# A two-block transformer kernel: in the bidirectional scan, the carried part of the output is scaled on ScalarE and the order of VectorE's work in a scan step is rearranged

## The reference, cut to what matters

```
cb     = einsum("bclgn,bcsgn->bcgls", cm, bm)
y_diag = einsum("bcgls,bcgels,bcsgep->bclgep", cb, exp(segsum(a)), xs)
y_off  = einsum("bclgn,bcgepn,bcgel->bclgep", cm, prev_states, exp(a_cs))
y      = y_diag + y_off
```

## Time and profile before

| | |
|---|---|
| median of three runs | 3659.97 us |
| the profiled execution: its time | 3656.11 us |
| its span, first to last instruction | 3654.3 us |
| TensorE busy | 3439.4 us (94%) |
| VectorE busy | 2409.4 us (66%) |
| ScalarE busy | 1713.0 us (47%) |
| GpSimd busy | 492.3 us (13%) |
| the eight full steps of the scan | about 1984 to 2195 us |

### The profile page before, as it was taken

The page is one execution under the profiler, slowest core; times in us unless marked ns, Lnnn a source line. Parts: engine busy times, 40 slices in busy tenths (PEclk is TensorE's granted clock), DMA queues, the critical chain, the costliest instruction groups (busy, mean ns, idle before and its releaser), DMA issues.

```text
span 3654.3 us, 43770 instructions
## 1 busy us (share of the span) xinstructions
PE 3439.4 (94%) x13658; PEld 2393.2 (65%) x13658; DVE 2409.4 (66%) x2948; ACT 1713.0 (47%) x2318; POOL 492.3 (13%) x630
## 2 busy tenths in 40 slices
PE   7989999999988999998998889989999999999996
PEld 3445588874344588875654554378887888888884
DVE  3565464553564464555556874179999999999995
ACT  2344232232344332233321113168888888888884
POOL 0000000000000000000000000024343433334340
PEclk9988999999988999999998999999999999999998
DMA  4100233332110233332111002169999999999995
GB/s 180 52 31 28 81 116 115 113 101 69 52 35 23 87 112 113 116 114 71 52 52 58 24 24 92 63 245 372 355 375 347 369 367 365 369 355 376 352 372 182
DMA packets 167697, 618.86 MB, mean 169 GB/s; under 512 B 18496, under 2 KB 18624, under 8 KB 166880
## 3 DMA queue, kind: packets, MB, share of 16 engines
q1 hardware_dynamic: 156768, 573.84, 43.7%
q0 software_dynamic: 10816, 43.52, 4.2%
HBM read 587.92 MB, written 29.36 MB: 169 GB/s over the span
## 4 chain that ended last, share of the span: by engine, by line
PE 53%; issue 21%; POOL 11%; DVE 9%; ACT 3%; POOLq 2%; DMA 1%; DVEq 0%; SPq 0%; ACTq 0%
PE bank L589 51%; POOL pick L555 2%; POOL sb_work L501 2%; POOL y_rows L561 1%; DVE sb_rstd L1737 1%; DVE sb_work L1779 1%; POOL sb_work L507 1%; POOL picks_e L508 1%; POOL sb_work L547 1%; POOLq L514 1%; POOL sb_work L549 1%; POOLq L513 1%; ACT sb_work L1327 1%; POOL sb_work L544 1%; DVE sb_work L2259 0%
## 5 line engine op out<-in xcount | busy, mean ns | idle before, releaser
L2462 DVE TENSOR_TENSOR w_part<-sb_ring,w_part 128x1024 fp32r<-128x1024 f32 x762 | 890.1, 1225 | 63.1 <-ACT w_part L1641 38.9
L1641 ACT ACTIVATE w_part<-sb_ring 128x1024 fp32r<-128x1024 f32 x762 | 770.5, 1054 | 80.5 <-PE bank L1126 47.7
L1126 PE MATMUL bank<-w_part,xg_hi 128*128 128x512 f32 x2048 | 564.1, 397 | 0.0
L589 PE MATMUL bank<-h_hi,split_part 128*128 128x512 f32 x1408 | 447.5, 403 | 4.8 <-ACT h_hi L1409 4.8
L1126 PEld LDWEIGHTS bank<-w_part,xg_hi 128*128 128x128 f32 x2048 | 383.1, 188 | 89.1
L589 PE MATMUL bank<-sb_work,sb_ring 128*128 128x512 f32 (+5 forms) x880 | 331.4, 531 | 4.0 <-ACT sb_rstd L1202 2.5
L1126 PE MATMUL bank<-w_part,xg_lo 128*128 128x512 f32 x1024 | 321.2, 395 | 0.0
L589 PEld LDWEIGHTS bank<-h_hi,split_part 128*128 128x128 f32 x1408 | 267.2, 191 | 69.2 <-ACT h_hi L1409 5.1
L1126 PE MATMUL bank<-w_part,act_hi 128*128 128x512 f32 x1024 | 284.9, 400 | 2.0 <-DVE act_lo L2505 0.9
L589 PE MATMUL bank<-sb_hT,sb_ring 128*128 128x512 f32 (+1 forms) x608 | 272.5, 606 | 9.6 <-ACT sb_hT L1218 9.6
L589 PE MATMUL bank<-h_lo,split_part 128*128 128x512 f32 x704 | 272.1, 393 | 0.0
(11 more groups left out here) (350 smaller groups left out, 4630.2 us busy)
## 6 DMA issues: line engine op xcount, KB each, us to landing
sb_ring<-in_w SPq DMA_DIRECT2D x768, 512.0 KB, 7.4
sb_ring<-in_wstream SPq DMA_DIRECT2D x304, 512.0 KB, 3.5
y_rows<-sb_padc POOLq DMA_DIRECT2D x1, 4096.0 KB, 27.4
sb_xT<-in_x SPq DMA_DIRECT2D x1, 2048.0 KB, 11.6
x_rows<-sb_padc SPq DMA_DIRECT2D x1, 2048.0 KB, 22.7
residual<-sb_hT POOLq DMA_DIRECT2D x1, 2048.0 KB, 6.6
sb_hT<-residual POOLq DMA_DIRECT2D x1, 2048.0 KB, 8.2
x_rows<-sb_work SPq DMA_DIRECT2D x1, 2048.0 KB, 7.0
```

The lines of the kernel that those rows point to most:

```text
L589: ins = nc.tensor.matmul(out, l, r, start=start, stop=stop)
L1126: ins = nc.tensor.matmul(out[n][:], l[:, k, :], r[:, n * 512:(n + 1) * 512], start=False, stop=(k, p) == (KD - 1, 2))
L1641: nc.scalar.activation(w_hi[t % SPLITS], ring[:, t % RING, :], ACT.Copy).then_inc(s_hi, 1)
L2462: nc.vector.tensor_tensor(w_lo[t % SPLITS], ring[:, t % RING, :], w_hi[t % SPLITS].bitcast(F32), ALU.subtract).then_inc(s_lo, 1)
```

## The change

The scaling of the carried part goes from VectorE to ScalarE. ScalarE's instruction takes a scale of one number for each partition, so one instruction scales one head (128x64): six instructions for a group in place of one, 24 in a step. They go into four places in place of two: two in `turn_tables`, two in `rstd`. On ScalarE, groups 0 and 1 are scaled after the exponentials of group 0, group 2 after those of group 1, and group 3 after those of group 2. On VectorE the addition stays (`add_carried`), and the order is new: seg_arg 2 comes ahead of decayed 1 and seg_arg 3 right after it, and the additions of the carried part stand among the others. The bank of a `yoff` is now freed by ScalarE. TensorE's order is the same.

```diff
-        yoffs = turn_tables[:, :, 0:GW]
+        yoffs = [a[:, i, 0:GW] for a in (turn_tables, rstd) for i in range(2)]
...
 (ScalarE, at the end of each group g)
+                        for q in ((0, 1), (2,), (3,), ())[g]:
+                            act.wait_ge(pe_done, when("full", "yoff", s, q))
+                            if s > 2 * CB:
+                                act.wait_ge(dve_done, when("carried", s - 1, q))
+                            for e in range(HPG):
+                                o, n = e * HEAD_W, d * SSD_HEADS + q * HPG + e
+                                act.wait_ge(act_done, did.n)
+                                nc.scalar.activation(yoffs[q][:, o:o + HEAD_W], bank_of("yoff", s, q)[:, o:o + HEAD_W],
+                                    ACT.Copy, scale=ecs[:, b, n:n + 1]).then_inc(act_done, did.up(
+                                    *([("free", "yoff", s, q), ("yoff_scaled", s, q)] if e == HPG - 1 else [])))
...
 (VectorE)
+                    def add_carried(g):
+                        yg = ytok[:, b, g * GW:(g + 1) * GW]
+                        dve.wait_ge(act_done, when("yoff_scaled", s, g))
+                        dve.wait_ge(dve_done, did.n)
+                        nc.vector.tensor_tensor(yg, yg, yoffs[g], ALU.add).then_inc(dve_done, did.up(("carried", s,
+                            g)))
+
                     seg_arg(0)
                     seg_arg(1)
                     decayed(0)
-                    for g in range(GROUPS):
-                        yg = ytok[:, b, g * GW:(g + 1) * GW]
-                        dve.wait_ge(pe_done, when("full", "yoff", s, g))
-                        dve.wait_ge(dve_done, did.n)
-                        nc.vector.tensor_tensor(by_head(yoffs[:, g % 2, :]), by_head(bank_of("yoff", s, g)[:, 0:GW]),
-                            per_head(ecs, blk, d, HPG, g * HPG), ALU.mult).then_inc(dve_done, did.up(("free", "yoff",
-                            s, g)))
-                        dve.wait_ge(dve_done, did.n)
-                        nc.vector.tensor_tensor(yg, yg, yoffs[:, g % 2, :], ALU.add).then_inc(dve_done, did.up())
                     seg_arg(2)
                     decayed(1)
+                    seg_arg(3)
+                    add_carried(0)
                     add_within(0)
-                    seg_arg(3)
                     decayed(2)
+                    add_carried(1)
                     add_within(1)
                     decayed(3)
-                    add_within(2)
-                    add_within(3)
+                    for g in (2, 3):
+                        add_carried(g)
+                        add_within(g)
```

## The result

The changed kernel took 3673.68 us (median of 7 runs, 3669.25 to 3677.05), the kernel before 3656.41 (7 runs, 3648.7 to 3660.52): ratio 1.0054, 95% interval 1.0044 to 1.0064. So it is slower, as forecast, but by 17 us between the two medians and 20 us by the ratio (14 against 3659.97, the median that the forecast started from), where 7.5 were forecast. A second timing of the same two gave 1.0048 (1.0031 to 1.0065).

A forecast was written before the change was run, and what follows sets the result against it. Bound: the chain through VectorE, TensorE and ScalarE to decayed 3, then a back half held by VectorE and TensorE. Steps +3.9 and clock falls +3.6 make +7.5 us on 3659.97: 3667.5, range 3650 to 3675.

The forecast's parts named there:

- ScalarE's price for a head: One 128x64 scaling out of PSUM on ScalarE: 315 ns each, 0.033 us between, as each waits for the last.
- ScalarE's chain and the bank of yoff 3 as the new end of the front half: From seg_arg 0's end to decayed 3's: scalings delay exponentials, TensorE waits for the bank; 0.79 us longer a step.
- S + 15.91: Forecast end of decayed 3, in us after the end of seg_arg 0 (S); before the change 15.12.
- The tail: VectorE after decayed 3: four additions in place of two, state's decay starts 2.64 us after it, not 2.23; +0.41.
- Sum of the undisturbed step: An ordinary full step of the scan takes 1.20 us more, 28.40 in place of 27.20.
- The falls: TensorE's clock dropping to 1.2 GHz around idle time: about as many as before, at some 70% of their price, 3.6 us.
- Rival 3: Clearly slower: a fall in most steps, each 2 us, or 348 ns a scaling; 3674 to 3678; chance 0.10.
- the 348 ns: Upper bound for one head's scaling on ScalarE in place of 315 ns: 0.8 us more a step, 3674.
- Rival 2: No change that can be told, within 0.2% (7.3 us); 3664 if the clock's falls don't come back; chance 0.37.
- Rival 1: ScalarE's short activations overlap, 0.22 us a head: a step 1.2 us shorter, eight make -10, 3650; chance 0.15.

The follow-up runs named there:

- `a_bank`: Changed kernel with two banks of the ring passed over ahead of group 3's segment product, so its halves don't wait for the scaling of group 3; 3672.54 us.
- the filled kernel: Changed kernel with TensorE doing the within-chunk product of group 1 twice, filling 1.3 us of its 2.27 us idle stretch; 3657.81 us, 1.0012 of the kernel before.

## Why the prediction was wrong

- **ScalarE's price for a head: right.** 315 ns and 0.348 us apart forecast; 314 ns, and twelve in 4.21 us, a twelfth of which is 0.351.
- **ScalarE's chain and the bank of yoff 3 as the new end of the front half: right.** Forecast S + 15.91 (+0.79) with a wait of about 2.4 us, measured S + 15.69 (+0.57) with 2.27. My leads of 0.15 us for a third wait were too long: between the last scaling and the next exponential stand 0.12 us at most. `a_bank` showed the bank's own share.
- **The tail: right.** +0.41 forecast, +0.45 measured: the state's decay starts 2.68 us after the last `decayed` in the undisturbed third step (2063.29 to 2065.97 in its timeline), before 2.23.
- **Sum of the undisturbed step:** +1.20 forecast; +0.99 measured in the filled kernel (28.19), +0.91 in the two distances of 28.11, whose step starts late.
- **The falls: this term failed.** "So I expect about as many falls of the clock, at some 70% of their price ... 0.7 x 5.1 = 3.6." There were six and not two, each 2.2 to 3.3 us: 12.2 in seven distances and some 2.9 in the eighth step, so 15 for 3.6. Less the two old falls (5.1), and with the longer steps (6.4 and 0.6), these are the 17 us by which the scan grew. I carried the count of two from the old step to the new one for no other reason than that its idle stretch is as long. The runs show that this isn't enough: one and the same stretch gave 2, 4, 8 and 4 falls in steps of other lengths. What sets the count stays open. The cover by ScalarE's chain hardly helps, because the low clock begins where that chain ends (2090.4, the last exponential from 2090.01 to 2090.50) and lies on the products behind it. Rival 3 had named it ("A fall in most steps", 3674 to 3678) with a chance of 0.10; that, less the 348 ns, is what came.
- **Rival 2** had for it that five of eight steps took the old wait without a fall; it was six, since the eighth step of the kernel before has none either.
- **Rival 1** was the right reading of the two chains of activations: with the waits as written the overlap isn't there, without them it is (0.23 us a head for the forecast's 0.22), and then the kernel is faster by 20 us and not its 10, since the falls go with it.

## What to carry to other kernels

When work goes to an idle engine in small pieces, each waiting on the one before it, price the wait with the piece: here 24 pieces with needless waits turned a gain of 20 us into a loss of as much. Look also at who waits for what the pieces release (here a PSUM bank, and behind it TensorE), and treat a wait of 2 to 3 us on TensorE in every round of a loop as a risk of its own: the number of falls of its clock that one kernel's trace shows did not carry over to any kernel here with a longer round. Fill such a wait with products, or take it away, before trusting the trace's count. And try the order of the busy engine's own work first: here it gave 10 us with nothing moved.

## What the runs showed of the hardware

- A run of activations in which each waits on the one before: 0.351 us apart at 0.314 us each; without the wait 0.232 apart (2.79 us for twelve).
- More products on TensorE made a kernel faster: 1.3 us of repeated products a step took 13 to 15 us off 3673.
- The same 2.5 us of idle TensorE (2.50 to 2.56 in all but one step) came with a fall of the clock (at 1.2 GHz, four segment instructions in 2.93 us and not 1.56) in 2, 4, 8 and 4 of 8 steps, as only the busy part of the step got longer.
- A fall began in the idle stretch (the seventh step of the kernel before: 0.68 in the window 2156.50 to 2157.00, TensorE idle to 2157.70) or behind it, by 1.3 us in the fourth step of the changed kernel.
- Idle time split into stretches of 1.45 and 1.17 us came with falls in 5 of 8 steps, split into 0.6, 0.55 and 1.7 in 8, split into 1.7 and 0.8 in 2; one stretch of 2.3 (and 0.6) had 6.
